# Projection rows for tiles 2 to 8 moved into tile 0's expert steps, the GLU into its attention, one program for startup and trunk

## What is computed

```python
z = x @ w_in                                # q | k | v | u, 512 columns each; k and v are outputs too
a = diff_attention(q, k, v)                 # 4 heads, two softmax maps each, ALiBi, causal
s, h = s5_mixer(u)                          # complex diagonal SSM: 32 groups of 16 channels, 64 states
                                            # y = gelu(...); s = y * sigmoid(y @ w_glu + b_glu)
x1 = layer_norm(ALPHA * x + concat(a, s) @ w_out)
q  = rms_norm(x1 @ w_q)                     # PEER: 8 heads, 2 x 128 keys
idx, g = top 16 of the 16 x 16 sums of the top 16 of each half; softmax
act = gelu(u_tab[idx] . x1);  f = sum((g * act) * v_tab[idx])     # 8 x 16 = 128 experts a row
y  = layer_norm(ALPHA * x1 + f)
```

## Time and profile before

| | us |
|---|---|
| median of 3 runs | 3808.65 (3800.52 to 3809.73) |
| the profiled execution | 3797.05, span 3795.2, mean granted clock 0.781 |
| PE, DVE, ACT, POOL busy | 2619, 2438, 1504, 1285 |
| DMA | 1308 MB, 345 GB/s over the span |
| first gather | 489.0 |
| first dots of tiles 0, 1, 2 | 509.8, 866.5, 1233.1 |

### The profile page before, as it was taken

One profiled execution on the slowest core, in us unless ns is written; L12 is line 12 of the kernel. 1 busy time (PEld: TensorE's weight loads), 2 busy tenths in 40 slices (PEclk: granted clock), 3 DMA queues, 4 the chain that ended last, 5 costly groups with the idle time before them and its releaser, 6 DMA issues.

```text
span 3795.2 us, 44329 instructions
## 1 busy us (share of the span) xinstructions
PE 2619.2 (69%) x14060; PEld 1083.0 (29%) x14060; DVE 2437.5 (64%) x5639; ACT 1504.0 (40%) x4355; POOL 1284.7 (34%) x1099
## 2 busy tenths in 40 slices
PE   7899466676677667766776676667757776457756
PEld 4578231132123212321231223122312332222311
DVE  8601386578557855875587659765966696335775
ACT  1111134444444444444443444354445444334433
POOL 0000034433443344334434543444344433112334
PEclk9999686787788777867886788688867877777866
DMA  5321389999999999999999999999999999788988
GB/s 142 87 79 49 128 355 398 419 371 386 406 381 411 368 414 375 402 382 414 374 396 382 408 373 390 397 410 376 385 393 411 374 379 397 287 304 315 399 333 340
DMA packets 240490, 1308.16 MB, mean 345 GB/s; under 512 B 41619, under 2 KB 69555, under 8 KB 90483
## 3 DMA queue, kind: packets, MB, share of 16 engines
q0 software_dynamic: 156672, 1140.92, 74.7%
q1 hardware_dynamic: 81890, 159.13, 12.2%
q10 hardware_dynamic: 1696, 5.27, 0.4%
HBM read 1285.65 MB, written 17.97 MB: 343 GB/s over the span
## 4 chain that ended last, share of the span: by engine, by line
DMA 29%; DVE 27%; PE 15%; issue 7%; ACT 7%; SPq 2%; POOL 2%; DVEq 0%; POOLq 0%
DMA UV<-in_peer_uv,icur 26%; DVE junk L1385 11%; PE psum L1051 8%; PE psum L977 3%; DMA wq<-in_cache_k 2%; POOL UV L881 2%; PE psum L997 2%; DVE sc L1292 2%; ACT D L1157 1%; DVE E L1352 1%; DVE E L1345 1%; ACT L1152 1%; ACT wge L1154 1%; SPq L817 1%; DVE it L1291 1%
## 5 line engine op out<-in xcount | busy, mean ns | idle before, releaser
L1051 PE MATMUL psum<-UV,D 64*64 64x512 f32 x8704 | 1544.8, 803 | 951.4 <-ACT D L1157 924.3
L881 POOL DMA_INDIRECT UV<-in_peer_uv,icur x1088 | 1279.2, 1176 | 2099.2 <-PE psum L1051 1823.5
L1385 DVE CUSTOM_DVE_ANT_0 junk<-UV,x 128x1024 bf16<-128x1024 f32 x1088 | 1333.8, 1226 | 774.7 <-DMA UV<-in_peer_uv,icur 702.3
L1152 ACT ACTIVATE ge<-acts 128x1 f32<-128x1 f32 x1088 | 219.7, 202 | 1622.3 <-DVE acts L1385 1621.3
L1051 PEld LDWEIGHTS psum<-UV,D 64*64 64x64 f32 x8704 | 318.5, 162 | 1884.6 <-issue 1850.3
L1157 ACT ACTIVATE D<-id,wge 128x64 f32<-128x64 f32 x1088 | 378.3, 348 | 35.4
L1154 ACT ACTIVATE wge<-ge,gcur 128x1 f32<-128x1 f32 x1088 | 320.5, 295 | 35.3
L997 PE MATMUL psum<-wq,aT 128*128 128x256 f32 (+1 forms) x1152 | 306.2, 425 | 1.2 <-ACT aT L1102 1.2
L997 PEld LDWEIGHTS psum<-wq,aT 128*128 128x128 f32 (+1 forms) x1152 | 234.6, 209 | 113.7 <-issue 65.7
L1152 ACT ACT_TABLE_LOAD x111 | 142.4, 1283 | 2.0
L308 PE MATMUL psum<-w_in_sb,xT 128*128 128x256 f32 (+1 forms) x576 | 130.7, 385 | 0.0
(11 more groups left out here) (297 smaller groups left out, 2354.0 us busy)
## 6 DMA issues: line engine op xcount, KB each, us to landing
wq<-in_peer_w_q SPq DMA_DIRECT2D x72, 1024.0 KB, 9.1
UV<-in_peer_uv,icur POOLq DMA_INDIRECT x1088, 10.1
wq<-in_cache_k SPq DMA_DIRECT2D x64, 256.0 KB, 9.0
vrows<-in_cache_v SPq DMA_DIRECT2D x64, 256.0 KB, 9.4
w_in_sb<-in_w_in SPq DMA_DIRECT2D x8, 1024.0 KB, 6.3
x<-in_x_all SPq DMA_DIRECT2D x9, 512.0 KB, 8.1
w_out_sb<-in_w_out SPq DMA_DIRECT2D x1, 4096.0 KB, 17.6
out<-x ACTq DMA_DIRECT2D x8, 512.0 KB, 8.5
```

The source lines that it names most:

```text
L881: pool.indirect_dma_start(out=UV[:, n % RING, :], out_offset=None, in_=table, in_offset=bass.IndirectOffsetOnAxis(ap=icur[:, t % 2, column ...
L1051: ins = pe.matmul(bank[6 + r][q:q + 64, :], D[64 * r:64 * r + 64, n % RING, :], UV[64 * r:64 * r + 64, n % RING, DM + 512 * e:DM + 512 * e ...
L1152: act.activation(ge[:, j:j + 1], acts[:, j:j + 1], ACT.Gelu).then_inc(sem("gelu_done"), 1)
L1385: dve.tensor_tensor_reduce(out=junk[:, :], in0=UV[:, n % RING, 0:DM], in1=x1[:, t % 2, :], scale=1.0, scalar=0.0, op0=ALU.mult, op1=ALU.ad ...
```

## The change

Startup and trunk become one block with one set of tiles that share zones of memory (`cut`): x_T and the SSM's large tiles lie in the slots of `UV`, in the home of w_out and of the layer-norm gains; the meeting of all engines between the two is gone. Only the K and V rows of tiles 0 and 1 (8 units) are left in the startup. The other 28 units (14 K, 14 V) are spread over tile 0's expert steps 14 to 81, one every 2.5 steps, in banks 1 and 3; their w_in blocks are loaded again into `wq`'s slots, ACT issues their output writes. The GLU's five blocks go into tile 0's four attention heads, through one buffer `sS`; tile 0 takes its s columns from `sS` by a copy. Tile 0 uses a copy of w_out (`w_tmp`) in the `UV` slots; w_out is loaded into its home after the last unit. The trunk's constants move into the SSM part of VectorE's list (`dve_constants`). Tile 0's expert steps begin after the first combination (head 0) instead of the second, its heads 1 to 7 shift by 4 front steps, and its first ten expert steps take two front steps each.

```diff
+        uvf = UV[:, :, :].rearrange("p s n -> p (s n)")
+        xTa = cut(uvf, 0, KC, 256)
+        bigA = cut(uvf, 2048, G * P)
+        EX = uvf[:, 6144:10240].rearrange("p (n i k) -> p n i k", n=2, i=GP)
+        w_tmp = cut(uvf, 2048, KC, DM)
+        xTb = cut(home, 0, KC, TR - 256)
+        st = cut(home, 6656, 3, 416)
+        tAB = cut(lngf, 0, 4, 8 * NCH)
+        sS = cut(lngf, 0, 4, 256)
+        gate = cut(lngf, 1024, 4, 256)
...
+        CHUNK = [(0, 256), (256, 416), (672, 416)]
...
+        W_END = [6, 12, 18, 24, 26, 28, 30, 32]
+        GBANK = (1, 3, 6, 7)
...
+            slot = wq[:, i % 3, :, :] if i % 3 < 2 else UV[:, RING - 1, :].rearrange("p (k n) -> p k n", k=KC)
...
+            sp.wait_ge(sem("ss_y"), GP // 3 + 1)
+            for j in range(L):
+                sp.dma_start(scr_y[:, :, j, :].rearrange("g c n -> c g n"), U[C * j:C * j + C, :, :])\
+                  .then_inc(sem("y_out"), 16)
...
+            sp.wait_ge(sem("ss_hs"), 1)
+            sp.dma_start(qT, scr_q[:, :, 0:P]).then_inc(sem("q_in"), 16)
+            sp.wait_ge(sem("ss_hps"), 1)
+            sp.dma_start(wg, a["ssm_w_glu"]).then_inc(sem("wg_in"), 16)
+            sp.wait_ge(sem("y_out"), 16 * L)
+            for q in range(4):
+                sp.dma_start(yT[:, q, :], scr_y[8 * q:8 * q + 8, :, :, :].rearrange("g c j n -> (g c) (j n)"))\
+                  .then_inc(sem("yT_in"), 16)
+            w_load(7)
+            sp.dma_start(keysT, a["peer_keys"]).then_inc(sem("keys_in"), 16)
+            sp.dma_start(w_tmp, a["w_out"][0].rearrange("(k p) n -> p k n", p=P)).then_inc(sem("w_tmp_in"), 16)
+            sp.wait_ge(sem("ss_hout"), 1)
+            for n in range(2):
...
+            for n in range(4):
+                blk, t = divmod(n, 2)
+                sp.wait_ge(sem("z_ev"), K_0 + n + 1)
+                sp.dma_start(k_rows[t * P:t * P + P, 256 * blk:256 * blk + 256], krow[:, n % 3, :])\
+                  .then_inc(sem(f"k_out{n % 3}"), 16)
...
+            for n in range(4):
+                blk, t = divmod(n, 2)
+                rows(K_0 + n, 4 + blk, t)
+                if n:
+                    k_columns(n - 1)
...
+            for n in range(4):
+                blk, t = divmod(n, 2)
+                rows(V_0 + n, 6 + blk, t)
+                if n == 0:
+                    k_columns(3)
+        def pe_glu(pe, b):
+            if b == 0:
+                pe.wait_ge(sem("ss_hout"), 1)
+                pe.wait_ge(sem("wg_in"), 16)
+                pe.wait_ge(sem("yT_in"), 64)
+            n0, nn = glu_block(b)
+            for q in range(4):
+                n = G0 + 4 * b + q
+                if b:
+                    pe.wait_ge(sem("z_ev"), n - 3)
...
+                last.then_inc(sem("z_ps"), 1)
+        def pe_unit(pe, i):
+            blk, t = divmod(i, 7)
+            t += 2
+            r = rows_of(t)
+            pe.wait_ge(sem(f"w3_in{blk % 2}"), 16 * (blk // 2 + 1))
+            if i in (0, 1):
+                pe.wait_ge(sem("z_ev"), G0 + 20)
+            elif i < 16:
+                pe.wait_ge(sem("k_Tcopied"), 4 + i - 1)
+            else:
+                pe.wait_ge(sem("r_ev"), i - 1)
+            x = x_columns(t * P, r)
+            for k in range(KC):
+                last = pe.matmul(bank[(1, 3)[i % 2]][:r, 0:256], x[:, k, :], wq[:, blk % 2, k, :], start=k == 0, stop=k == KC - 1)
+            last.then_inc(sem("r_ps"), 1)
...
+        def pe_unit_columns(pe, i):
+            r = rows_of(2 + i % 7)
+            pe.wait_ge(sem("r_ev"), i + 1)
+            for c in range(2):
+                last = pe.transpose(bank[(1, 3)[i % 2]][:, c * P:c * P + r], krow[:r, (4 + i) % 3, c * P:(c + 1) * P], ident[:r, :r])
+            last.then_inc(sem("k_T"), 1)
...
+                if n == 3:
+                    act.wait_ge(sem("k_out0"), 16)
+                    act.wait_ge(sem("k_T"), 1)
+                act.activation(krow[:, n % 3, :], bank[(K_0 + n) % 4][:, 0:256], ACT.Copy).then_inc(sem("z_ev"), 1)
...
+        def act_glu(act, b):
+            nn = glu_block(b)[1]
+            if b == 0:
+                act.wait_ge(sem("bg_in"), 16)
+            for q in range(4):
+                n = 4 * b + q
+                act.wait_ge(sem("z_ps"), G0 + n + 1)
+                if b:
+                    act.wait_ge(sem("gl_mul"), n - 3)
+                act.activation(gate[:, q, 0:L * nn], bank[GBANK[q]][:, 0:L * nn], ACT.Sigmoid, bias=bg[:, q:q + 1])\
+                   .then_inc(sem("z_ev"), 1)
...
+        def act_unit(act, i):
+            blk, t = divmod(i, 7)
+            t += 2
+            r = rows_of(t)
+            act.wait_ge(sem("r_ps"), i + 1)
+            src = bank[(1, 3)[i % 2]][:r, 0:256]
+            if blk < 2:
+                n = 4 + i
+                act.wait_ge(sem(f"k_out{n % 3}"), 16 * (n // 3))
+                act.wait_ge(sem("k_T"), n - 2)
+                row = krow[:r, n % 3, :]
+                dst, name = (k_rows[t * P:t * P + P, :] if t < NT else ks_rows), f"k_out{n % 3}"
+            else:
+                row = vrows[:r, t, 256 * (blk % 2):256 * (blk % 2) + 256]
+                dst, name = (v_rows[t * P:t * P + P, :] if t < NT else vs_rows), "v_out"
+            act.activation(row, src, ACT.Copy).then_inc(sem("r_ev"), 1)
+            act.wait_ge(sem("r_ev"), i + 1)
+            act.dma_start(dst[:, 256 * (blk % 2):256 * (blk % 2) + 256], row).then_inc(sem(name), 16)
...
+            dve.wait_ge(sem("h_out"), 64)
...
+        def dve_constants(dve, step):
+            dve.wait_ge(sem("gain_in"), 32)
+            tmp = lngf[:, 0:SEQ]
+            dve.wait_ge(sem("T_in"), 16 * L)
+            step(dve.tensor_scalar(tmp, bias[:, 0:SEQ], 0.0, MASKED, ALU.is_gt, ALU.mult))
+            step(dve.tensor_tensor(bias[:, 0:SEQ], bias[:, 0:SEQ], tmp, ALU.add))
...
+        def dve_glu(dve, b):
+            n0, nn = glu_block(b)
+            for q in range(4):
+                dve.wait_ge(sem("z_ev"), G0 + 4 * b + q + 1)
+                if q == 0 and b:
+                    dve.wait_ge(sem("s_out"), 16 * b)
+                    dve.wait_ge(sem("sT_copied"), 1)
+                last = dve.tensor_tensor(sS[:, q, 0:L * nn].rearrange("p (n j) -> p j n", j=L),
+                                         yT[:, q, :].rearrange("p (j n) -> p j n", j=L)[:, :, n0:n0 + nn],
+                                         gate[:, q, 0:L * nn].rearrange("p (j n) -> p j n", j=L), ALU.mult)
+                last.then_inc(sem("gl_mul"), 1)
+            if b == 0:
+                dve.wait_ge(sem("gl_mul"), 4)
+                dve.tensor_copy(sT, sS[:, :, 0:P]).then_inc(sem("sT_copied"), 1)
+        def dve_unit_columns(dve, i):
+            blk, t = divmod(i, 7)
+            t += 2
+            r = rows_of(t)
+            dve.wait_ge(sem("k_T"), 4 + i + 1)
+            dve.tensor_copy(kT[:, 2 * blk:2 * blk + 2, t * P:t * P + r],
+                            bank[(1, 3)[i % 2]][:, 0:256].rearrange("p (h t) -> p h t", h=2)[:, :, :r])\
+               .then_inc(sem("k_Tcopied"), 1)
...
+        def sp_heads(sp, t):
             for e in range(EH):
                 wait(sp, "q_ps", 8 * t + e - 1)
+                if t == 0 and e < 2:
+                    wait(sp, "z_ps", W_END[6 + e])
+                if t == 1 and e < 2:
+                    wait(sp, "r_ps", 21 + 7 * e)
                 sp.dma_start(wq[:, e % 2, :, :], a["peer_w_q"][order(t)[e]]).then_inc(sem(f"wq_in{e % 2}"), 16)
+                if t == 0 and e == 1:
+                    sp_first(sp)
                 if t == NT and e == EH - 2:
...
+        def sp_first(sp):
+            for b in range(5):
+                n0, nn = glu_block(b)
+                sp.wait_ge(sem("gl_mul"), 4 * b + 4)
+                sp.dma_start(scr_s[:, :, L * n0:L * (n0 + nn)], sS[:, :, 0:L * nn]).then_inc(sem("s_out"), 16)
+            sp.dma_start(x1[:, 0, :], a["x_all"][0:P, :]).then_inc(sem("xin"), 16)
+            sp.wait_ge(sem("s_out"), 80)
+            for n, name in enumerate(("ln1_g", "ln1_b", "ln2_g", "ln2_b")):
+                sp.dma_start(lng[:, n, :], a[name][0, :].partition_broadcast(P)).then_inc(sem("ln_in"), 16)
+        def sp_rest(sp):
+            for j in range(2):
+                sp.wait_ge(sem("q_ps"), 7 + j)
+                sp.dma_start(wq[:, j, :, :], a["w_in"][BLOCKS[4 + j]]).then_inc(sem(f"w3_in{j}"), 16)
+            sp_front(sp, 1)
+            for j in range(2):
+                sp.wait_ge(sem("r_ps"), 7 * j + 7)
+                sp.dma_start(wq[:, j, :, :], a["w_in"][BLOCKS[6 + j]]).then_inc(sem(f"w3_in{j}"), 16)
+            sp.wait_ge(sem("r_ps"), 28)
+            sp.dma_start(w_out, a["w_out"][0].rearrange("(k p) n -> p k n", p=P)).then_inc(sem("w_out_in"), 16)
...
-                wait(pe, "sT_in", 16 * t + 16)
-                wait(pe, "w_out_in", 16)
+                if t:
+                    wait(pe, "sT_in", 16 * t)
+                    wait(pe, "w_out_in", 16)
+                else:
+                    wait(pe, "sT_copied", 1)
```

(40 more changed lines are left out.)

1157 lines of the change are left out of this document (530 added, 627 removed).

## The result

The changed kernel takes 3769.73 us (median of 4 runs, 3766.05 to 3773.69), where the kernel before took 3809.02 beside it: ratio 0.9902, interval 0.9884 to 0.9921, so 30 to 44 us less. The forecast was 3749, 60 us less: the sign and the range are right, a third of the gain is missing. The profiled run took 3767.13 (span 3765.3), 29.9 less than the profiled run of before (3797.05); the rest of this text compares these two traces.

What follows compares the result with a forecast made beforehand. Transfers, with VectorE spells, bound the body; a TensorE and VectorE chain bounds the head before the first gather. Head -125 and tile 0 +65 net -60 against the median 3808.65: 3749 us, range 3700 to 3790.

Steps and rivals of the forecast that it cites:

- HP and TensorE's start: Head, early VectorE chain: constants add 6.9 us ahead of the SSM's scan; the state is ready at 182.8.
- The y products: Head, on TensorE once the state is ready: they take 34.7 us and end at 217.5.
- rival C: Tile 0's units: TensorE stays at 1.2 GHz, its work doubles; tile 0 pays 209, total 3893; chance 0.04.
- SP's queue and ScalarE's wait: Head: ScalarE's K row 3 copy waits for k_out(0), queued behind reads of 21 to 23 us; scores at 271.
- rival B: Head: the SP queue doesn't hold k_out(0) back; 18 us less, total 3731; chance 0.1.
- Attention with GLU: Head, tile 0's attention: a head takes 9.2 us instead of 5.5 with a GLU block; ends at 311.7.
- Output stage, head 0, combination: End of the head: output stage 31.6 less 1.2, to 342; then 21.8 to the first gather at 364.
- step 16: Tile 0, steps 0 to 15, VectorE-bound: step 16 comes at +69 instead of +63.9 after the first gather, +5.
- steps 16 to 49: Tile 0's K units: a loop through the engines sets the pace, 129 us against 85.2 + 2.5, +41.
- 49 to 81: Tile 0's V units: VectorE does not wait; about 90 us against 80, +10.
- Rival A: Tile 0: the units hide and only added transfers are paid, +34; total 3718; chance 0.17.
- Rival D: Head: SP's list of waits holds something placed too early; 30 us less gain, total 3779; chance 0.09.

Runs made afterwards that it cites:

- experiment 5: The changed kernel with SyncE's reads of the key tables and w_tmp issued behind the first three K outputs: 3756.18 us, ratio 0.9866 to the kernel before.
- Experiment 6: The changed kernel with VectorE's copy of a unit's transposed K columns one expert step later: 3740.37 us, ratio 0.9836 to the kernel before.
- Experiment 3: The changed kernel with 16 unused products of 256 columns put after the first six of 32 pairs of y product groups: 3758.55 us, ratio 0.9886.
- experiment 4: The kernel before with twelve more VectorE copies ahead of HP, leaving TensorE idle 2.70 us before the y products: 3836.58 us, ratio 1.0085.
- experiment 2: The changed kernel with eight unused products of 256 columns on TensorE ahead of its wait for HP: 3749.36 us, ratio 0.9858 to the kernel before.
- experiment 1: The changed kernel with VectorE's constants (7.0 us) written behind the diagonal operand HP instead of before it: 3739.58 us, ratio 0.9836 to the kernel before.

## Why the forecast was right in sign and too large

The ledger of the first gather (forecast 364, measured 389.97, so 26 us):

- **HP and TensorE's start.** Forecast 182.8, measured 180.1: 2.7 us better. The constants took 7.0 (forecast 6.9), and the wait for T ended 2.7 us earlier than in the trace of before (128.47 against 131.13 in the earlier trace rows).
- **The y products: the step that failed.** The forecast took 34.7 us from the earlier trace rows and put it behind an idle time that it had itself worked out (HP at 182.8, TensorE ready at 181.1: 1.7 us). The idle time was there, 2.17; what it does to the products behind it was costed at nothing. It is 61.0 us: 26.3 missing. The forecast asked about the clock in rival C, for the K units in the body, where the trace grants 0.92 and 0.98, and not here, where 34.7 us of work follow that didn't lift the level. The earlier trace rows is at 1.00 for these products because nothing was idle ahead of them; the duration and the clock belong to that context.
- **SP's queue and ScalarE's wait.** From the end of the y products to the scores of head 0: forecast 53.5, measured 56.5. The y reads follow the first scr_y write by 16.3 us (forecast 16.0), and the eviction of K row 3 comes 26.5 after those reads (forecast 24.2). Right in kind; experiment 5 shows that 11 us of the wait hang on the two large reads, of 5.2 MB, which the forecast's 0.41 MB/us prices at 13; rival B had 18 for the whole queue.
- **Attention with GLU.** Head to head 8.75 us (scores at 297.58, 306.33, 315.07, 323.82), forecast 9.2. From the scores to the output stage's transposes 42.8 (forecast 40.7).
- **Output stage, head 0, combination.** 27.7 and 21.8 us, forecast 30.4 and 21.8.

The sum of the differences: -2.7 + 26.3 + 3.0 + 2.1 - 2.7 + 0 = 26.0.

The forecast named a sign of its being wrong: "if the head's end moves by less than 100 us, or if later tiles take longer than 371". The first gather moved by 99.0 (488.96 to 389.97), so the first half of it came true, by 1 us. The tiles behind take up to 371.1, as the kernel before has them at up to 371.4: that half says nothing. Its other signs came as said, apart from the first gather's own time: the idle of ScalarE ahead of the fourth K eviction (28.9 us, ended by a transfer), the heads' distance, the pairs of dots in the K units, the clock above 0.85.

The body, from the first gather: step 16 at +70.5 (forecast 69), steps 16 to 49 in 129.8 (129), 49 to 81 in 87.2 (90), the rest in 158.7 (155: the 148.5 + 9 of the forecast count from step 80, and one step of 2.5 is in the 33 steps of the K units already); 446.2 against 442.5. The sum is closer than its parts: the forecast spread 9 us of VectorE's work and 6 of slow products over the K units, and in the trace their first half, with spells at the low level and more of VectorE's own work, is slower than its 7.6 and 8.9 and the second half close to them. Rival A, the units hidden, would have had 412: refuted by the trace. Experiment 6 shows that it was one step of VectorE's order away from being nearly true. Rival C is refuted too (the K units at 0.92, the V units at 0.98), though single units ran at the low level (0.50 from 479 to 485). Rival D had the head's gain 30 us smaller for a queue that holds something back. The head did gain 26 less, but not for that reason; a right number there would have been luck.

The forecast set its -60 against the median of before. The traces differ by 29.9, the medians by 39.3, and the interval spans both; I read nothing into the 9 us between them. So the ledger accounts for the 30 us that are missing between the traces; by the medians 21 are missing.

On the Trainium skill's sentence that I had set against rival C: TensorE: Matmul & The Clock Gate, "What's actually happening", calls the throttled state the default which activity releases. The y products of the change are against the plain reading of it: 59 us of work at 0.50 with no idle time, and no release. Experiment 3's wide products did release it.

## What to carry to other kernels

When a change delays TensorE's operand, look at what stands behind the idle time it makes: a couple of microseconds cost 26 here, because 34.7 us of products followed that stayed at the low level. That they are narrow is not the reason by itself: products of 128 columns were followed by the high level in the kernel before (experiment 4). So take a duration from a row only together with the idle time ahead of it and the clock in it. If such an idle time can't be removed, fill it with products, as experiment 2 did with eight of 256 columns, or put a burst of them in behind it: a burst of 9.4 us brought the first dot forward by 10. And where work is interleaved into a loop that hands over between engines, let each consumer run one step later than its producer needs: that single number was worth 30 us, while cutting seven eighths of TensorE's 3.7 us per unit gained 0.7 us in all the V units together.

## What the runs showed of the hardware

- An idle time of 2.17 us (2.70 in experiment 4) with the clock at 1.00 was followed by 0.50 about 2 us after work had resumed; 0.61 us (experiment 2) and none (experiment 1) were not. In the K units of the change 2.57 us were too, there before the work resumed.
- At 0.50, TensorE stayed there through 59 us of y products with no gap; a burst of 32 recorded products of 256 columns on 128 rows brought back 1.00 in under 9.4 us, and so did the first K row in the change (between 5 and 6 us into it). In the kernel before, 64 recorded products of 128 columns, 6.6 us long, started at 0.50 too, and the level was 0.94 in 110 to 112, as they ended.
- In steps 16 to 49 of experiment 6 the DMA engines were busy 0.97 of the time and TensorE 92%. Cutting 3 MB of writes left these steps at 99.9 us against 100.3: a DMA share near 1 is not by itself the bound.
- A small write issued by SyncE right behind reads of 5.2 MB took 7.52 us to issue, ahead of them 0.59 (experiment 5).
